# Fourteen fused gathers among the last V groups, and one retrieval unit ahead of the last sums

## The reference, cut to what matters

```python
def peer(x, w_query, sub_keys, expert_u, expert_v):
    q = (xt @ w_query).reshape(T, PEER_HEADS, 2, PEER_D_HALF)
    s = jnp.einsum('thcd,hckd->thck', q, sub_keys)
    top_s, top_i = lax.top_k(s, PEER_TOPK)
    ...
    best_s, pos = lax.top_k(cand_s, PEER_TOPK)
    expert_idx = jnp.take_along_axis(cand_i, pos, axis=-1)
    gate = jax.nn.softmax(best_s, axis=-1)
    ...
        u = jnp.take(expert_u, ic, axis=0)
        h = jax.nn.gelu(jnp.einsum('cd,ced->ce', xc, u))
        vv = jnp.take(expert_v, ic, axis=0)
        return jnp.einsum('ce,ced->cd', gc * h, vv)
```

## Time and profile before

| | |
|---|---|
| median of 3 runs | 1688.07 us (1684.24 to 1688.5) |
| the profiled execution's own time | 1698.7 us |
| its span, first to last instruction | 1696.9 us |
| TensorE busy | 1292.9 us (76%) |
| VectorE busy | 1170.3 us (69%) |
| POOL busy | 628.7 us (37%) |
| ScalarE busy | 264.6 us (16%) |
| transfers | 603.45 MB, mean 356 GB/s |
| granted TensorE clock, mean | 0.88 |

### The profile page before, as it was taken

How to read it: one execution, slowest core, us unless ns; L and a number is a source line. 1 busy time by engine, 2 the same in 40 slices (tenths; PEclk the granted TensorE clock), 3 DMA queues, 4 the chain that set the end, 5 groups by cost and what they waited for, 6 DMA issues and landing times.

```text
span 1696.9 us, 11942 instructions
## 1 busy us (share of the span) xinstructions
PE 1292.9 (76%) x3440; PEld 623.6 (37%) x3440; DVE 1170.3 (69%) x2831; ACT 264.6 (16%) x748; POOL 628.7 (37%) x677
## 2 busy tenths in 40 slices
PE   7678998936287996458787777777888778697786
PEld 3556445613133563123333333333333333233332
DVE  1428999788956795698767676867676777664554
ACT  0110000022111111012121212121221212121111
POOL 0002425333543745734343333333334333343330
PEclk9989998957597998779897889989888898889998
DMA  7768869775867988999999999999999999999992
GB/s 255 282 223 324 324 235 349 281 247 198 294 229 269 337 321 287 388 421 422 422 421 421 421 422 421 422 422 421 421 421 422 421 422 422 421 421 421 422 421 111
DMA packets 125663, 603.45 MB, mean 356 GB/s; under 512 B 12576, under 2 KB 14880, under 8 KB 76320
## 3 DMA queue, kind: packets, MB, share of 16 engines
q0 software_dynamic: 92160, 536.91, 78.9%
q1 hardware_dynamic: 33440, 65.80, 10.8%
HBM read 600.57 MB, written 2.10 MB: 355 GB/s over the span
## 4 chain that ended last, share of the span: by engine, by line
DMA 37%; PE 27%; DVE 24%; issue 6%; POOL 2%; ACT 2%; another core or an unknown queue 1%; ACTq 0%; SPq 0%; POOLq 0%; DVEq 0%
DMA arena<-uv,idx 33%; PE W L469 7%; PE W L501 5%; DVE arena L1005 5%; DVE arena L962 4%; PE ACC L469 4%; PE W L507 3%; DMA arena<-uv,stage 2%; POOL arena L406 2%; PE W L677 2%; PE ACC L450 2%; PE X L649 1%; DMA arena<-w_in 1%; DVE cand L1243 1%; DVE cand L1245 1%
## 5 line engine op out<-in xcount | busy, mean ns | idle before, releaser
L469 PE MATMUL W<-arena,diag 128*128 128x512 f32 x1024 | 502.5, 652 | 150.9 <-ACT diag L902 150.9
L434 POOL DMA_INDIRECT arena<-uv,idx x384 | 363.8, 947 | 584.3 <-PE W L469 372.0
L1005 DVE SCALAR_TENSOR_TENSOR arena<-arena,X 128x1024 f32<-128x1024 f32 x256 | 309.0, 1219 | 198.1 <-DMA arena<-uv,idx 197.3
L469 PEld LDWEIGHTS W<-arena,diag 128*128 128x128 f32 x1024 | 210.3, 209 | 443.1 <-issue 256.4
L406 POOL DMA_INDIRECT arena<-uv,stage x256 | 256.1, 1000 | 294.1 <-DVE arena L962 139.2
L469 PE MATMUL ACC<-arena,diag 128*128 128x512 f32 x512 | 253.0, 656 | 71.3 <-ACT diag L902 71.2
L1005 DVE SCALAR_TENSOR_TENSOR arena<-arena,W 128x1024 f32<-128x1024 f32 x128 | 154.8, 1219 | 95.3 <-DMA arena<-uv,idx 94.8
L469 PEld LDWEIGHTS ACC<-arena,diag 128*128 128x128 f32 x512 | 106.2, 211 | 218.1 <-issue 130.7
L902 ACT ACTIVATE diag<-ident,gate 128x128 f32<-128x128 f32 x384 | 123.2, 390 | 355.2 <-DVE gate L1012 349.8
L501 PE MATMUL W<-arena 128*128 128x512 f32 x320 | 143.7, 606 | 12.8 <-DMA ident<-ident_in 11.6
L962 DVE SCALAR_TENSOR_TENSOR arena<-arena,X 128x1024 f32<-128x1024 f32 x128 | 148.6, 1215 | 1.2 <-DMA arena<-uv,stage 0.7
(11 more groups left out here) (190 smaller groups left out, 904.9 us busy)
## 6 DMA issues: line engine op xcount, KB each, us to landing
arena<-w_in SPq DMA_DIRECT2D x14, 2048.0 KB
arena<-peer_w_query SPq DMA_DIRECT2D x8, 2048.0 KB
arena<-w_out SPq DMA_DIRECT2D x4, 2048.0 KB
arena<-uv,idx POOLq DMA_INDIRECT x384, 29.3
arena<-uv,stage POOLq DMA_INDIRECT x256
out<-xs SPq DMA_DIRECT2D x4, 512.0 KB
arena<-xT SPq DMA_DIRECT2D x1, 1536.0 KB, 11.9
xs<-x SPq DMA_DIRECT2D x1, 1536.0 KB, 14.3
```

Source lines behind the costliest of these rows:

```text
L434: pool.indirect_dma_start(out=fused[slot], out_offset=None, in_=uv, in_offset=bass.IndirectOffsetOnAxis(ap=idx[:, E + n:E + n + 1], axis=0 ...
L469: last = nc.tensor.matmul(sum_of(b)[:, half * HW:(half + 1) * HW], fdiag[:, n % ND, :], fused[n % NS][:, D + half * HW:D + (half + 1) * HW ...
L1005: STT(out=fused[slot][:, 0:D], in0=fused[slot][:, 0:D], scalar=1.0, in1=token_of(b), op0=ALU.mult, op1=ALU.mult, accum_out=hid[:, E + n:E ...
```

## The change

On POOL, the loop over the fused gathers becomes a function `pairs(lo, hi)` with the same waits; gathers 0 to 5 are issued behind V group 9, 6 to 9 behind group 13, 10 to 13 behind group 14, and the rest behind group 15 as before. On VectorE, `retrieve(1, 1)` moves from behind the last sums to between halves 23 and 24. In the changed kernel the lines behind are 9 higher.

```diff
-            for i in range(V_GROUPS):
-                n = AT_V + i
-                one_table(D, i * RING, n, n % 2)
-            for n in range(NF):
+            def pairs(lo, hi):
+                for n in range(lo, hi):
+                    pair(n)
+
+            def pair(n):
                 slot = n % NS
...
+            after = {9: (0, EARLY), 13: (EARLY, 10), 14: (10, LATE)}
+            for i in range(V_GROUPS):
+                n = AT_V + i
+                one_table(D, i * RING, n, n % 2)
+                if i in after:
+                    pairs(*after[i])
+            pairs(LATE, NF)
...
-            scored = 17
-            sums(taken[0] - 2 * U_GROUPS, scored)
+            scored = (17, 24)
+            sums(taken[0] - 2 * U_GROUPS, scored[0])
             retrieve(1, 0)
-            sums(scored, 2 * V_GROUPS)
-
+            sums(scored[0], scored[1])
             retrieve(1, 1)
+            sums(scored[1], 2 * V_GROUPS)
+
```

## The result

The changed kernel took **1691.76 us** in the median of 8 runs (1687.74 to 1695.26), the kernel before 1686.01 on the same chip (8 runs): ratio 1.0026, 95% interval 1.0015 to 1.0036, so about 4 us *slower* (by the two medians alone it would be 5.75 us). Run again later it was 1690.31 (12 runs) against 1687.29: 1.0017, 1.0006 to 1.0028. Both times lie inside the range and both ratios inside the 0.3% that I had called no change. But neither interval contains 1, and both stand on the other side of zero from my 1.5 us of gain.

What follows compares the result with a forecast made beforehand. The DMA queue, full at 421 GB/s, bounds the kernel: 20.8 us of old holes against 18.4 us of new ones gives 2.4 us, taken as 1.5 us off the 1688.07 us median: 1686.5 us, range 1675 to 1694.

Steps and rivals of the forecast that it cites:

- my 1.5 us of gain: Whole kernel: 2.4 us earlier by the walk, taken as 1.5 us; chance 0.62 of staying within 0.3%.
- The 21 us of holes before: Queue between 618.5 and 703.5 in the kernel before: 20.8 us of empty time, all the change can win there.
- group 12 row 5: First new hole, 5.1 us: POOL's issue waits for TensorE, which adds row 3 of group 11 10.8 us later.
- group 13 row 0: Second new hole, 5.7 us: POOL's issue waits for VectorE, which does the moved retrieval ahead of group 12.
- gather 18: Third new hole, 5.1 us: it waits for the first fused pair to be added and is issued at 745.1.
- The rival of the stretched retrieval: Moved retrieval takes 22.7 us instead of 15.7, the hole at group 13 grows by 7: 1693.5 us, chance 0.13.
- The sum: Whole ledger: new holes 5.1 + 5.7 + 1 + 5.1 and about 1.5 = 18.4 us against 20.8, 2.4 us earlier.
- those come free while group 15 lands, so they follow: Gathers 14 to 17: their ring rows come free in time, so the queue stays full until 743.4.
- 1.7 us from a faster TensorE: At gather 18: TensorE, idle only some 5 us, may run at its upper clock level, giving back up to 1.7 us.
- Group 9 and the 40 us of full queue: About 1.5 us of hole at the start, group 9's own; queue full from groups 13 to 15 on.
- mostly in TensorE's part, which the change keeps: Walk of the profile's own stretch on the same prices: a few us short, put down mostly to TensorE's part.
- 0.47 us for each issue: VectorE's loss per POOL issue beside the retrieval, from 7.0 us for 15 issues; 1.5 us for three.

Runs made afterwards that it cites:

- retrieval alone: Kernel before with only retrieve(1, 1) moved ahead of half 24, all fused gathers left behind group 15: 1689.82 us, ratio 1.0011 to before.
- gathers alone: Changed kernel with retrieve(1, 1) put back behind the last sums, gathers moved as changed: 1705.25 us, ratio 1.0097 to before; 1703.43 us when run again.
- the best one: Changed kernel with TensorE's rows behind the query, retrieve(1, 1) ahead of half 20, gathers 10 to 13 behind group 15 again: 1675.95 us, ratio 0.9937 to before.

## Why the prediction was right and wrong

**Right: what bounds, and that the change is a ledger.** The table above is that statement, tried on ten kernels. The range held. The largest chance, 0.3% or less, held by the ratio (1.0026), but not as I had put it, as no change that can be told: eight runs of each kernel told it.

**Right: the places.** The 21 us of holes before, the new ones at group 12 row 5, group 13 row 0 and gather 18, and a full queue in the 20 us ahead and the 40 us in between (412, 415 and 416 GB/s). The rival of the stretched retrieval did not come: it took 15.7 us, 653.96 to 669.70, while POOL issued 4 gathers (and ended a fifth).

**Wrong: the sum, by 6.6 us of new holes, and with it the sign.** The step that failed is the subtraction of "The sum": it takes new holes that were walked with shortest waits, 18.4 us, from old ones that were measured, 20.8. From 1.9 us behind the issue on I had 18.4 us of new holes; the rows show 2.5 + 15.5 + 0.5 + 6.5 = 25.0 (each 20 us less bytes / 421 GB/s, in the first 40, the next 40, the next 40, the last 20). The terms that were too small:

- Groups 12 and 13: 11.8 us forecast, 15.5 measured. The retrieval began 1.9 us late (653.96 is 662.9 on the clock of before, against 661), and POOL's wait behind it ended 1.8 us late. Then I gave the eight rows of group 13 one microsecond of loss at 1.33 to 1.4 us apart; POOL took 10.5 us for the seven steps from 671.90 to 682.36, 1.5 apart. It waited for no slot there; the issues themselves were longer (rows below).
- Gathers 15 to 19: 5.1 us forecast, 6.5 measured. The failing sentence is "those come free while group 15 lands, so they follow". Gather 15 waited 3.54 us for TensorE, whose 12 matmuls for group 15 took 8.41 us, against 5.32 us for 12 at 670.79, when it had been busy: after 12.10 us of idling its granted clock was 0.50 from 720 to 730, the 1.2 GHz level. Gather 18 is issued at 741.38, 750.4 on the clock of before, where I had 745.1. I had even hoped for 1.7 us from a faster TensorE there, and its first 16 matmuls took 8.83 us against 8.70. So part of this hole lies ahead of gather 18, at a place that the prediction didn't name: 298 GB/s from 730 to 735, where gathers 15 and 16 had come late.
- Group 9 and the 40 us of full queue: 1.5 us forecast, 2.5 + 0.5 measured.

Of the first seven issues of group 13, which took 1.00 to 1.43 us each behind an idle time of 0.30, the 5th to 7th are these (timeline of POOL):

```profile
677.52 1.32 POOL L406 DMA_INDIRECT arena<-uv,stage  x1 [0.30 <-issue]
679.14 1.43 POOL L406 DMA_INDIRECT arena<-uv,stage  x1 [0.30 <-issue]
680.88 1.17 POOL L406 DMA_INDIRECT arena<-uv,stage  x1 [0.30 <-issue]
```

In group 14 (689.82 to 698.54), while VectorE had nothing to sum, the issues took 0.94 to 0.96 us. What lengthens them was not tried.

I had seen that my walk ran short on the profile of before, and waved it through as "mostly in TensorE's part, which the change keeps". On the changed kernel it ran short by 6.6 us. How I explain it, and no run tries this apart: waits that were hidden before stand open when the queue runs dry, and each shortest price is then missing once. That all ends are shortest waits is a bias of one sign, and should have moved the centre to 0 or above.

**The stretched retrieval.** On the Trainium skill's page SBUF — State Buffer (section SBUF: two separate sides) a two-port operation of VectorE keeps GpSimd from writing descriptors. No run here shows POOL's issues late beside the retrieval. VectorE's loss of 7 us in the kernel before (its x15 are 14 issues begun beside the retrieval and the end of one) has come in no other profile: with 4 issues beside it (changed kernel and retrieval alone) and 2 (gathers alone) the retrieval took 15.7 to 15.8 us, and with 8, those of group 10 where it stands at half 20, 16.0 us. By 0.47 us for each issue, eight would have cost 3.8 us; so that estimate of mine falls. In the kernel before the 7 us are pauses ahead of eight of VectorE's instructions, the first of 1.67 us, and hardly any instruction took longer:

```profile
712.13 0.69 DVE L1220 TENSOR_TENSOR cand<-best_v 128x512 f32<-128x512 f32 x1 [1.67 <-remote]
...
718.41 0.09 DVE L1229 MATCH_VALUE_LOAD top_p<-top_v,cand 128x8 f32 x1 [1.31 <-DVE top_v L1228]
```

What made them was not tried. They came beside fused gathers, and the eight issues beside row gathers; that difference stays open.

## What to carry to other kernels

Where one queue sets the end, write the ledger of its holes, and move work into it only together with the stock it takes out elsewhere: the gathers gained 5 us where they were put and cost 6.6 where they had been the cover. Waits that stand in a row on one in-order queue are worth little one at a time (1 to 3 us) and a lot together (8 to 11 us), so an edit that changes nothing is not yet refuted. Put the long, movable piece of work (here a retrieval) where its engine is starved by the very transfers just inserted; here that paid once TensorE's wait behind it was gone too (1690.49 to 1680.54 us), and hardly before (1690.23).

## What had not been expected of the hardware

The last gathers end on a small part of the DMA engines. In the last 11 us before the last dot the share is 0.16 at 67 GB/s in the changed kernel, and 0.09 at 37 GB/s in the best one, while VectorE still waits 1.2 us for each gather and gets one every 2.46 us, as at full rate:

```profile
1658.00:1669.20 11.20, 8.45 (x20) 3.53 (x19) 5.18 (x11) 1.49 (x5) 0.00 (x0) 1.00 0.16 67
```

```profile
1664.34 1.22 DVE L1014 SCALAR_TENSOR_TENSOR arena<-arena,X 128x1024 f32<-128x1024 f32 x1 [1.15 <-DMA arena<-uv,idx]
...
1666.80 1.22 DVE L1014 SCALAR_TENSOR_TENSOR arena<-arena,X 128x1024 f32<-128x1024 f32 x1 [1.23 <-DMA arena<-uv,idx]
...
1669.26 1.22 DVE L1014 SCALAR_TENSOR_TENSOR arena<-arena,X 128x1024 f32<-128x1024 f32 x1 [1.23 <-DMA arena<-uv,idx]
```

```profile
1641.60:1652.60 11.00, 8.25 (x14) 3.37 (x13) 4.99 (x9) 1.49 (x5) 0.00 (x0) 0.71 0.09 37
```

The rate over these 11.2 us of the changed kernel, in 40 slices of 0.28 us (view of the transfers), shows how it ends:

```profile
GB/s 263 293 263 263 205 146 176 88 88 117 59 29 29 29 29 29 29 29 29 29 29 0 29 29 29 29 29 29 29 29 29 29 0 29 29 29 29 29 0 0
```

29 GB/s is one packet of 8 KB in a slice. The packets in the trace follow one another singly there, some 0.31 us each, where 16 and more are in flight in mid-stream, and one packet at a time is what one engine moves (8 KB in 0.31 us is 26 GB/s, and 421 / 16 is 26.3). So fifteen of the engines were done 7 us before the slowest in the changed kernel, 9 us in the best one and 10 us in the kernel before (0.10 at 41 GB/s from 1664 to 1675.5). It is in all three that were looked at, so it doesn't touch the comparison; where that lag comes from was not tried.
